# Eight projection steps ahead of the first delta head, the value taps ahead, and the gate's projection partly in its own head

## What is computed

```python
proj = h @ w_in                                    # h is rms-normed x
qkv = silu(causal_depthwise_conv(proj[..., :3 * DN_WIDTH], conv_w))   # 4 taps
z = proj[..., 3 * DN_WIDTH:4 * DN_WIDTH]           # the gate
q, k, v = split(qkv, 3); q, k = l2_normalize(q), l2_normalize(k)      # per head
# chunks of 64: decay from g; sol = triangular_solve(lower + eye, [v*beta, k_beta*exp(gc)])
def step(state, inp):
    v_new = u_c - w_c @ state
    o_c = q_c @ state + a_c @ v_new
    state = state * gl + k_c.T @ v_new
    return state, o_c
o = o * rsqrt(mean(o * o) + eps) * norm_w * silu(z)
y = o @ w_out
```

## Time and profile before

| | us |
|---|---|
| median of 3 runs | 3102.67 (3102.61 to 3103.27) |
| span of the profiled execution | 3102.1 |
| PE busy | 2953.6 (95%) |
| PE weight loads | 2445.9 (79%) |
| DVE busy | 1820.8 (59%) |
| ACT busy | 1210.9 (39%) |
| POOL busy | 901.7 (29%) |
| start of the first head's transposes | 81.8 |
| start of the last head's | 672.0 |

### The profile page before, as it was taken

The page is one execution under the profiler, slowest core; times in us unless marked ns, Lnnn a source line. Parts: engine busy times, 40 slices in busy tenths (PEclk is TensorE's granted clock), DMA queues, the critical chain, the costliest instruction groups (busy, mean ns, idle before and its releaser), DMA issues.

```text
span 3102.1 us, 37785 instructions
## 1 busy us (share of the span) xinstructions
PE 2953.6 (95%) x14715; PEld 2445.9 (79%) x14715; DVE 1820.8 (59%) x2359; ACT 1210.9 (39%) x1929; POOL 901.7 (29%) x684
## 2 busy tenths in 40 slices
PE   7899999989999999999998999999989999999997
PEld 6688888878788888888876777888878778887886
DVE  7566566564365544333366886554574866666866
ACT  5555555553311112221334776222332444444222
POOL 5333332221000000000302886331331444443423
PEclk9999999999999999999999999999999999999999
DMA  3111111112143333111210001011023144446953
GB/s 128 41 48 48 48 48 48 42 62 102 41 129 110 111 113 102 48 48 54 93 53 21 11 9 49 28 35 35 21 75 149 40 157 150 148 148 239 371 207 122
DMA packets 96833, 274.00 MB, mean 88 GB/s; under 512 B 9232, under 2 KB 31248, under 8 KB 92176
## 3 DMA queue, kind: packets, MB, share of 16 engines
q1 hardware_dynamic: 96656, 271.58, 25.0%
HBM read 208.43 MB, written 60.36 MB: 87 GB/s over the span
## 4 chain that ended last, share of the span: by engine, by line
PE 81%; DVE 10%; ACT 4%; issue 3%; POOL 1%; DMA 1%; SPq 0%; POOLq 0%; DVEq 0%; ACTq 0%
PE ps L663 25%; PE ps L1756 11%; PE ps L3068 11%; PE ps L3729 9%; PE ps L3096 7%; DVE b L3677 2%; PE ps L2659 2%; PE ps L1060 1%; DVE b L652 1%; PE ps L2466 1%; PE ps L2437 1%; PE ps L2465 1%; PE ps L1067 1%; PE ps L2480 1%; PE ps L90 1%
## 5 line engine op out<-in xcount | busy, mean ns | idle before, releaser
L663 PE MATMUL ps<-b 128*128 128x512 f32 x3912 | 1009.6, 403 | 29.7 <-DVE b L652 14.4
L663 PEld LDWEIGHTS ps<-b 128*128 128x128 f32 x3912 | 711.4, 191 | 159.2 <-issue 20.1
L1756 PE MATMUL ps<-b 128*128 128x512 f32 x1536 | 361.7, 396 | 0.6 <-DVE b L1924 0.6
L1756 PEld LDWEIGHTS ps<-b 128*128 128x128 f32 x1536 | 288.0, 188 | 69.5 <-DVE b L1924 1.0
L3729 PE MATMUL ps<-b 128*128 128x512 f32 (+1 forms) x1464 | 326.1, 377 | 6.3 <-ACT b L3788 5.9
L3729 PEld LDWEIGHTS ps<-b 128*128 128x128 f32 x1464 | 253.8, 191 | 55.6 <-issue 10.6
L644 ACT ACTIVATE b<-b 128x1024 fp32r<-128x1024 f32 x138 | 145.2, 1054 | 319.5 <-PE ps L1756 242.3
L3121 ACT ACTIVATE b<-b 128x512 fp32r<-128x512 f32 x232 | 142.3, 615 | 270.9 <-PE ps L3096 106.3
L652 DVE TENSOR_TENSOR b<-b 128x1024 fp32r<-128x1024 f32 x138 | 174.2, 1264 | 107.6 <-ACT b L644 98.5
L3068 PE MATMUL ps<-b 128*128 128x512 f32 x960 | 225.9, 393 | 6.0 <-DVE b L3371 3.8
L3068 PEld LDWEIGHTS ps<-b 128*128 128x128 f32 x960 | 180.5, 189 | 48.3 <-DVE b L3371 7.7
(11 more groups left out here) (372 smaller groups left out, 5011.4 us busy)
## 6 DMA issues: line engine op xcount, KB each, us to landing
inner<-b SPq DMA_DIRECT2D x77, 512.0 KB, 2.6
b<-inner SPq DMA_DIRECT2D x35, 1024.0 KB, 13.5
b<-in_down SPq DMA_DIRECT2D x52, 512.0 KB, 4.3
b<-in_mod SPq DMA_DIRECT2D x96, 256.0 KB, 2.6
b<-scratch SPq DMA_DIRECT2D x46, 512.0 KB, 4.4
b<-in_gu SPq DMA_DIRECT2D x44, 512.0 KB, 4.1
b<-in_dn_in SPq DMA_DIRECT2D x32, 512.0 KB, 4.9
b<-in_up SPq DMA_DIRECT2D x32, 512.0 KB, 3.7
```

The costliest lines, as they stand in the source:

```text
L663: ins = e.matmul(ps[:, c], w, h[:, k, c], start=first and k == 0 and i == 0, stop=last and k == KT - 1 and i == 2)
L1756: ins = e.matmul(ps[:, c], w, u[:, at[k], c], start=k == 0 and p == 0, stop=k == n - 1 and p == 2)
```

## The change

It consists of five edits, all in the delta stage and its start.

- `side.ahead(8)` runs the first eight pieces of unit 4 (head 1's queries), with what its `unit` asks of ACT and DVE, before the halves of head 0 on PE, ACT and DVE.
- In the start the weight split of unit 4 stands before the exponential `kdf` on ACT and before the key taps on DVE; on ACT the eviction of the values (`done(2, 0, 2)`) comes before the sigmoid of beta, and the first value tap before the silu of the keys.
- DVE does the value taps 1 to 3 at the end of its start; the list of taps in `DeltaSide` keeps only tap 4, in its third place.
- Of the gate's 16 pieces of head h only `early = 16 * (7 - h) // 7` are allowed in head h-1 (13, 11, 9, 6, 4, 2 and 0 for heads 1 to 7), the others in head h itself. They have to be through by the last step of its recurrence.
- In head 7 the second half fills in two of three rounds after the fifth, where it was one of three.

```diff
-        self.taps = [(0, 2, t) for t in range(1, 5)]
+        self.taps = [None, None, (0, 2, 4)]
...
     def project(self, h, which):
         j = 4 * h + which
-        self.on.unit(j)
-        for k in range(KT):
-            self.on.piece(j, k, 0)
-            yield None
-            self.on.piece(j, k, 1)
+        early = 16 * (H1 - 1 - h) // (H1 - 1)
+        for step in range(2 * KT):
+            if which == 3:
+                while self.head < h and step >= early:
+                    yield "idle"
+            if step == 0:
+                self.on.unit(j)
+            self.on.piece(j, step // 2, step % 2)
             yield None
...
+    def ahead(self, n):
+        for _ in range(n):
+            next(self.steps)
...
-            if self.taps:
-                h, which, t = self.taps.pop(0)
-                self.on.tap(h, which, t)
-                if t == 4:
-                    self.ready.add((h, which))
+            tap = self.taps.pop(0) if self.taps else None
+            if tap:
+                self.on.tap(*tap)
+                if tap[2] == 4:
+                    self.ready.add(tap[0:2])
...
         on.tap(0, 1, 0)
+        self.act_weights(e, 5)
         e.wait_ge(*V.at("g5"))
         e.activation(self.kdf, self.g2, ACT.Exp).then_inc(*A.up("kdf"))
-        self.act_weights(e, 5)
+        on.done(2, 0, 2)
         e.activation(self.beta, gt[:, :, 0:8], ACT.Sigmoid).then_inc(*A.up("beta"))
         on.tap(0, 0, 4)
+        on.tap(0, 2, 0)
         on.tap(0, 1, 4)
-        on.done(2, 0, 2)
-        on.tap(0, 2, 0)
         on.done(3, 0, 3)
...
+        self.dve_weights(e, 5)
         on.tap(0, 1, 1)
         on.tap(0, 1, 2)
         on.tap(0, 1, 3)
-        self.dve_weights(e, 5)
...
         e.tensor_tensor(d3, d3, self.each(self.con("later")), ALU.add).then_inc(*V.up("dd"))
+        on.tap(0, 2, 1)
+        on.tap(0, 2, 2)
+        on.tap(0, 2, 3)
...
             side.head = h
+            if h == 0:
+                side.ahead(8)
             side.until(h, 1)
...
-                elif turn < 5 or turn % 3 == (0 if f else 2):
+                elif turn < 5 or turn % 3 in ((2,), (2, 0))[f]:
                     side.fill(1)
```

## The result

The changed kernel took 3124.44 us (median of 4 runs, 3123.55 to 3128.83) beside 3102.97 (3102.61 to 3104.97) for the kernel before, measured along with it: 1.0071 times as long, interval 1.0056 to 1.0086. It is 21.5 us slower, where 2.5 us less were forecast, and lies outside the range.

The account below looks back on a forecast made before the run. PE, busy 95% of the span, was taken as the bound, so only its idle or half-clock time could go. 8.9 - 5.9 - 0.5 = 2.5 us saved, so 3102.7 - 2.5 = 3100.2 us; range 3092 to 3108.5.

Parts of the forecast that it names:

- (e): Ladder's first transposes, heads 1 to 6: the query group's new place gives 4.7 us back; 0.5 lost for the keys.
- part 3: Heads 1 to 6: five things change place, together 5.9 us lost, with bounds of 0 and 13.
- Part 1: Opening up to the x1 transposes: 12.8 us saved, less 1.0 charged for the clock behind a new wait of 2.95.
- Rival C: Opening gives little: the wait moves to the first product, 6 us instead of 2.95; about 3106 us; chance 0.10.
- Part 2: Rest of head 0: ladder waits 2.3 us against 5.8; tail loses 5.2, and the clock 1.2.
- (a): Ends of heads 3 to 6: value taps delay the gated product; 1.9, 3.6, 1.2, 1.2 us lost, 1.4 for clock.
- (b): Ladder of heads 3 to 5: the gate's eviction with its table load costs 1.2 + 1.3 + 1.5 us.
- (c): Recurrence of heads 4 to 6: the keys' unit change moves in and costs 2.2 us.
- (d): Recurrence of heads 1 to 6: the value group leaves it, giving 5.4 us back.
- Part 4: Head 7: waits of 3.5 and some 5.9 us, clock 2.4, 12.4 against 12.2 before; one more ladder tile, 0.5 lost.
- B: Whole kernel slower: (a) to (c) in full, more clock falls, half of (d) and (e); 3107 to 3110 us; chance 0.13.
- A: Hand-backs hide: ladder slack takes up (a) to (c), (d) and (e) come in full; 3093.7 us; chance 0.27.

Follow-up runs that it names:

- opening-only kernel: The changed kernel with every gate piece in its old place and the old rounds of head 7: 3101.62 us, ratio 0.9997.

## Why the prediction was wrong

The step that failed is the price of DVE's moved instructions in the ladder, (e) of part 3 above all: they were priced by their time alone and placed by the order of PE, ACT and DVE, without POOL. Where 4.7 us were to come back, 5.4 more were lost. The table splits the rest.

| us, against before | forecast | measured |
|---|---|---|
| opening up to the x1 transposes | -11.8 | -12.7 |
| rest of head 0 | +2.9 | +8.6 |
| heads 1 to 6: idle in the ladder | -0.2 | +8.3 |
| heads 1 to 6: idle where a head begins | +7.9 | +7.4 |
| heads 1 to 6: idle in the recurrence | -3.2 | -0.4 |
| heads 1 to 6: half clock | +1.4 | +5.5 |
| head 7 | +0.5 | +1.5 |

The measured idle times are from the waits views: ladder 20.3 us against 12.0 before, recurrence 8.3 (9.0 less 0.7 in head 0) against 8.6, by single gaps -0.4; the ladder of before is the 10.5 of rows 7 and 1.5 at L1082. They make 15.3 where the windows give 15.0, since short waits are not all listed. The half clock is what is left of the 20.5: PE's busy time in heads 1 to 6 is 468.5, before 472.1 less 9.1 of moved work. PE's idle time from 160 to 672, for which some 27 us were forecast, was 40.1.

**Part 1, the opening: right.** The x1 transposes began at 98.86 (forecast 98.7), after 52 long matmuls; the gap before L1030 was 2.71 (forecast 2.95). The clock was not lost there, so the 1.0 charged for it fell away. Rival C, a wait of 6 us, fell.

**Part 2, the rest of head 0: the sign was right, the size wrong.** The ladder's waits were to be 2.3; gaps of 2.74, 1.18 and 2.84 make 6.8, and the clock, down for 3.4 us behind the last, some 1.7 more. The prediction went through DVE's and ACT's order alone and priced a tap at 1.2 wherever it stood. Of these gaps, making the passes short takes away the 2.84, and sending both groups of taps back (in the opening-only kernel) takes away all three. The tail was smaller than charged: 2.8 as its one long wait (forecast 3.1) and 1.1 in the steps before it, where 5.2 in all, and 1.2 for the clock, were charged. That the clock stayed up there was luck of this execution: behind the same gap it fell in five others.

**Part 3 (a) and (b): right.** Where heads 4 to 6 begin, forecast 1.9, 3.6, 1.2 and 1.2, measured 1.68, 3.63, 1.20 and 0.90. In the ladder of heads 3 to 5, forecast 1.2, 1.3 and 1.5, measured 1.05, 1.20 and 1.50. The first of these, ACT and then PE, head 3 of after:

```profile
353.48 1.28 ACT L3642 ACT_TABLE_LOAD   x1
354.77 1.03 ACT L3642 ACTIVATE b<-ps 128x1024 f32<-128x1024 f32 x1
```

```profile
357.07 0.44 PE L1054 MATMUL ps<-b 128*128 128x128 f32 x2 [1.05 <-ACT b L1191]
```

The eviction starts 0.01 us after the table load ends, and PE waits 1.05 us for what stands behind it. The rule of the Trainium skill (ScalarE: Activation LUTs, What ACT_TABLE_LOAD costs), with a drain of 1.38 us beside each load, would have made each of these waits about that much longer; the trace disagrees, and going by the row was right.

**Part 3 (e): the step that failed most.** It took 4.7 us back for the query group, as its new place stands after the second product of a level. (Its own prices give less: three heads at 1.5 less 0.2 make 3.9.) It was worked out from PE, ACT and DVE, whose steps are dealt out together; POOL is not in that order. In heads 2 and 3 the new place is that of POOL's decay passes, and the group waits 4.3 and 4.0 us instead of 1.5 and 0.2. Over heads 1 to 6 it waits 2.5, 4.3, 4.0, 0.7, 1.2 and 1.7 us, 14.4 where the forecast left 4.3 (six times 1.5 less 4.7): 10.1 more, nearly the whole of the excess idle. 7.5 of it are shown to be the meeting with the passes: 3.46 and 2.84, gone with short passes and with moved ones, and head 5's 1.21, gone with short ones. The rest was not taken apart by a run. In head 6 it is not the meeting: POOL is idle and the three taps take 1.28 to 1.29 us. In head 1 the taps take 1.27 and 1.28, but two copies ahead of them took 1.98 beside passes of POOL (at 200.85), otherwise 0.41. The trace of before had warned: six of its 72 taps took 2.3 us, one in each of heads 1 to 6, beside a POOL pass that began 0.05 us earlier, but hidden.

**Part 3 (c) and (d): too small and half wrong.** The keys' unit change cost 1.36, 0.95 and 0.95 in the recurrence of heads 4 to 6 and 0.3 in short waits, where 2.2 in all were charged, net of what it had cost before. The value group did leave the recurrence in the later heads; but in heads 1 and 2 its unit change stands there still, two or three steps later than before: in head 1 a weight split (1.23 us) and the norm's reduction (0.68 and 0.16) are ahead of L1371 on DVE, and PE waits 1.85 us at L1132, in head 2 1.86, where the whole group had cost 0.95 and 0.49. The recurrence gave 0.4 back, not 3.2:

```profile
244.96 0.49 PE L1132 MATMUL ps<-b 128*128 128x128 f32 x2 [1.85 <-DVE b L1371]
```

**The clock: mis-sized.** One fall was charged in heads 1 to 6; there were four. Windows of after, columns as in rows 2, behind gaps of 2.78 (at 172), 1.85 (245), 3.46 (298), 1.86 (334) and 2.84 (385):

```profile
172.00:175.00 3.00, 2.92 (x24) 2.79 (x25) 1.67 (x4) 1.09 (x2) 0.00 (x0) 1.00 0.22 86
245.00:248.00 3.00, 3.00 (x12) 2.61 (x13) 2.37 (x4) 2.19 (x2) 0.00 (x0) 0.56 0.00 0
...
300.00:302.00 2.00, 2.00 (x9) 1.70 (x8) 0.00 (x0) 0.90 (x4) 0.00 (x0) 0.50 0.00 0
334.40:337.40 3.00, 3.00 (x20) 2.59 (x21) 2.01 (x4) 0.00 (x0) 0.44 (x1) 1.00 0.03 5
384.80:387.80 3.00, 2.97 (x13) 2.77 (x14) 0.75 (x3) 2.05 (x6) 0.00 (x0) 0.59 0.00 0
```

Behind three of the five the granted clock is near 0.5, which is 1.2 GHz, for about 3 us. The fourth fall is behind the 3.63 in head 5. Together they cost 5.5 us.

**Part 4, head 7: right.** Two gaps, forecast 3.5 and 5.9, measured 4.01 and 5.16 (PE, after):

```profile
690.36 1.09 PE L1037 MATMUL ps<-b 128*128 128x128 f32 x4 [4.01 <-ACT b L3661]
...
712.86 1.34 PE L1054 MATMUL ps<-b 128*128 128x128 f32 x4 [5.16 <-DVE b L1325]
```

Both lowered the clock, as charged. The excess is 1.0, of which a gap of 1.08 at L1132 is the likely cause; no run tested it. (The working's own terms, 3.5, 5.9 and 2.4, make 11.8 and not the 12.4 that it wrote.)

**The rivals.** B had the right side, at 3107 to 3110, and its point of decision, more than one fall of the clock, was passed. But its mechanism, (a) to (c) in full with only half of (d) and (e), was not the cause: (a) and (b) came as in the sum, and (e) became a loss. A fell: (d) and (e) brought nothing. (B's 14.1 is (a), (b) and (c) without the 1.4 for the clock that it names with them; with it B would come out 1.4 us slower.)

**The signs.** Neither of the two signs that were to show the forecast wrong came: the idle time from 160 to 672 rose, and the opening up to the x1 transposes was 12.7 us cheaper. The sign that mattered, idle time far above 27 us, was not among them.

## What to carry to other kernels

When DVE's work is moved by a few steps, lay POOL's timeline beside the new place and price each moved instruction by what it took beside a POOL pass, not alone; here the surprise lay with the engine that was missing from the written order. A cheap gain at one place (12.7 us in the opening) was kept here only when what it drags along was sent back to its old place: the opening alone saved 3.8 us of the stage with the taps early and 11.2 with the taps late. Test the halves of a change apart first; here one was worth keeping once its taps stood late, and the other was the whole loss. And compare stages head by head: a difference that lies in heads with equal steps was the clock's here, not the edit's.

## What was unexpected of the hardware

**DVE and POOL take turns, an instruction at a time.** A tap with two inputs in SBUF (128x1024) takes 1.27 us alone and 2.95 beside a POOL pass of 1.91 that began 0.05 earlier; a weight split 2.53 instead of 1.22; a copy of 128x128 2.37 instead of 0.22; and POOL's pass 3.21 instead of 2.39. DVE's ladder instructions with one input in PSUM kept their 0.28 and 0.42 us in the middle of a pass (at 129.1 to 129.9 of after, where POOL is busy from 128.2 to 131.4). The Trainium skill says so (SBUF — State Buffer, Who interferes with whom): "A DVE instruction with two SBUF inputs contends with a GpSimd instruction that reads SBUF", and copies can as well, with the loser blocked for the whole instruction. The traces agree.

**The length of a gap alone did not decide on the clock.** In the stage of after it fell behind all six gaps of 2.84 us and more, and behind one of 1.85, but not behind three of 2.71 to 2.78, nor behind one of 1.86. PE's order does not decide it either. Behind the gap of 2.78 at the end of head 0, where the clock stayed up in after, it fell in the five other executions that have it, four of them with after's instructions on PE, as here with the gated product first:

```profile
172.42:175.42 3.00, 3.00 (x14) 3.00 (x15) 0.75 (x1) 1.00 (x2) 0.00 (x0) 0.50 0.09 37
```

Behind the gap of 3.14 in that place it fell in three of four. What else decides was not tested.
